# Keys and values ahead of the queries, swaps between query units, angle reduction on GpSimd

## The chip, the cores and the metric

The kernel runs on one core of a Trainium2 chip. The metric is the device time of one execution in microseconds (us); several executions are timed and the median is given. The core has TensorE (PE in the rows; matmuls and, as PEld, weight loads), VectorE (DVE), ScalarE (ACT), GpSimd (POOL), SyncE (SP, whose queue here only issues transfers), and 16 DMA engines between HBM and the on-chip SBUF. TensorE writes to PSUM; no instruction of GpSimd in this kernel has an operand there.

## The reference, cut to what matters

Two transformer blocks on 256 tokens of width 1024, all in float32. The first block is a latent attention plus gated convolution, then a mixture of 32 experts; the second is a recurrent layer, a stick-breaking attention, an MLP and a gate. Only the attention of the first block is touched:

```python
z = hp @ w_in
c_q, c_kv, k_pe, gate_b, gate_c, x_in = jnp.split(z, SPLITS, axis=-1)
q = (rms_norm(c_q, q_norm) @ w_uq).reshape(bsz, plen, N_HEADS, QK_NOPE + QK_ROPE)   # 8 heads, 64 + 32
q_rope = apply_rope(q[..., QK_NOPE:], cos[:, :, None, :], sin[:, :, None, :])
kv = (rms_norm(c_kv, kv_norm) @ w_ukv).reshape(bsz, plen, N_HEADS, QK_NOPE + V_DIM) # 64 + 64
k_nope, v = kv[..., :QK_NOPE], kv[..., QK_NOPE:]
k_rope = apply_rope(k_pe, cos, sin)
attn = causal_block_attention(q_nope, q_rope, k_nope, k_rope, v)
```

cos and sin are those of position times frequency, for 16 frequencies and 272 positions (16 meta tokens and 256 tokens).

## The kernel before, in words

Every engine runs its own program in order; semaphores order the engines against each other. There is no planner: the order of work on each engine is written out by hand.

Weights come as slabs of up to 1 MB into a ring of 12 SBUF slots, in the order of the list SLABS1 (SP's queue, L443 to L462). A slab is cut into units. For each unit ScalarE copies the weights rounded to fp32r into WH (`high1`, L613), VectorE writes the remainder into WL (`low1`, L1061), and TensorE multiplies high by high, high by low and low by high (`triple`, L1741 to L1743). There are four unit buffers, so `high1` of a unit waits until TensorE has used the unit four before it. The result of a unit lies in a PSUM bank, `bank1`, and ScalarE takes it out (`take1`, L626). A column unit holds 128x1024 weights and takes 24 matmuls; a query unit holds one head, 128x192, and takes 6.

The first 8 units are columns of w_in: 0 and 1 are c_q, 2 is c_kv, 3 is k_pe, 4 to 7 are gate_c. Before, units 8 to 15 are the eight query heads and unit 16 is w_ukv. After them the units WOVEN (17) and up, the rest of w_in, are woven into the attention loop.

The order around the change, before:

- TensorE: units 0 to 7 (L1803), among them the matmul of the rope angles into PSUM bank 6 (L1807) and the swap of k_pe (L1818). Then the eight query units (L1822), `swap_queries(0)` (L1838: a matmul with a signed permutation of the rope halves for two heads, L1835), the key matmuls of heads 0 to 3, swaps 1 to 3, the keys of heads 4 to 7, three value tiles (L1860 to L1862), and the attention loop (L1905 to L1921).
- ScalarE: the takes of units 4 to 7, the sine table load and `rope_table(0)` (L695) inside them, then eight times `high1` and take of a query head with `rope_table(1)` in front of the third take, then eight copies of keys (L721), three of values (L725), then the exponentials.
- VectorE: `low1` of the units; `reduce_angle(0)` (L1151 to L1159: eight small instructions on 32x272, each waiting for the one before it) between `low1(5)` and `low1(6)`; the two norms; `low1` up to 10; `reduce_angle(1)`; `low1` of 11 to 16; the rope of the keys into all eight heads (L1186 to L1189); then `rope_queries(j)` (L1202 to L1204), one for each pair of heads, with `low1(WOVEN)` to `low1(WOVEN+2)` and the first steps of the softmax (L1248 to L1256) between them.
- GpSimd: constants and small transfers in its first 14 us, then nothing until the attention is done (L560).

Of the kernel before, what the change touches and what calls it, by code (L numbers as in the profile page):

```python
# [11 lines left out]
ALU = mybir.AluOpType  # L12
# [41 lines left out]
SLABS1 = [("cq", 2), ("kv", 2), ("gc0", 2), ("gc1", 2), ("uq", 8), ("ukv", 1),  # L54
# [12 lines left out]
def bank1(u_no):  # L67

    return u_no % 4 if u_no < WOVEN else 2 + u_no % 2
# [51 lines left out]
def build(nc, A, out):  # L121

    ctx = ExitStack()
    with ctx:
# [7 lines left out]
        def const(name):  # L132
# [4 lines left out]
            vector=("router_low", "kpe_sines", "mix_root", "ffn_in_root", "logits_by_feature", "group_centred", "chosen_ready", "pair_diff",  # L137
                    "overflow_known", "lambda_abs", "ple_root"),
            scalar=("router_high", "mix_std", "group_exp", "pair_exp", "lambda_exp"),
# [100 lines left out]
        ang_k = ar(5520, T)  # L240

# [266 lines left out]
        def _(pool):  # L508
# [35 lines left out]
            g.memset(rank_or[:], -1.0).then_inc(ev("pool_const"), 1)  # L544
            pool.dma_start(gain_pc[:], A["pre_ffn_norm"][0].rearrange("(p c) -> p c", c=DC))\
# [6 lines left out]
            for name, n in VEC2:  # L552
                v = A[name] if name == "norm_final_g_2" else A[name][0]
                if len(v.shape) == 2:
                    v = v.rearrange("k n -> (k n)")
                pool.dma_start(vrow2[row:row + n, :], v.rearrange("(c p) -> c p", p=P)).then_inc(ev("vec2_loaded"), 16)
                row += n

# [42 lines left out]
        def _(act):  # L601
# [59 lines left out]
            for t in range(TT):  # L661
# [4 lines left out]
                if t == 0:  # L666
                    act.wait_ge(ev("meta_square"), 1)
                    s.activation(xs(1, 2)[0:META, :], xs(0, 2)[0:META, :], ACT.Sqrt, scale=1.0 / D, bias=EPS)\
                        .then_inc(ev("meta_std"), 1)
# [9 lines left out]
            for k, dst in enumerate((cq[:, 0, :], cq[:, 1, :], ckv, kpe)):  # L679
# [8 lines left out]
                if k == 2:  # L688
                    root_of_mean("cq", S)
# [8 lines left out]
            for k in range(4):  # L698
# [5 lines left out]
                if k == 1:  # L704
                    rope_table(0)
# [3 lines left out]

            u0 = FIRST1["uq"]  # L710
            for k in range(HEADS):
                high1(u0 + 3 + k)
                if k == 2:
                    rope_table(1)
                take1(u0 + k, qcat[0:QD, k, :], rows=QD, n=S, scale=SCALE1)

            for h in range(HEADS):
                act.wait_ge(ev("nope_keys"), h + 1)
                if h == 0:
                    act.wait_ge(ev("rope_table"), 2)  # L720
# [5 lines left out]
            high1(WOVEN + 2)  # L726
# [318 lines left out]
        def _(dve):  # L1045
# [56 lines left out]
            def scaled(srcs, gains, n):  # L1102
# [11 lines left out]
                                   ALU.add, xs(0, 2)[0:META, :]).then_inc(ev("meta_square"), 1)  # L1114
            dve.wait_ge(ev("pos_loaded"), 16)
            v.tensor_scalar(pos_row[0:1, META:T], pos_int[0:1, :], float(META), None, ALU.add)\
                .then_inc(ev("pos_ready"), 1)
# [3 lines left out]
            dve.wait_ge(ev("meta_std"), 1)  # L1121
# [15 lines left out]
            two_pi = 2 * math.pi  # L1137
            p1 = 6.28125
            p2 = float(np.float32(np.round((two_pi - p1) * 2 ** 20) / 2 ** 20))
            p3 = two_pi - p1 - p2  # L1140
            magic = 1.5 * 2 ** 23
            lim = 3.1415925
            rows = slice(NOPE, QD)
            angp = ps[rows, 6, 0:T]
            kr_a = rope_a[rows, 0:T]

            def reduce_angle(k):
                dst = (ang_k, ang)[k]
                turn = 0.25 * k
                tmp = rstd[rows, 0:T]  # L1150
                chain(v.tensor_scalar(tmp, angp, 1 / two_pi, turn, ALU.mult, ALU.add))  # L1151
                chain(v.tensor_scalar(tmp, tmp, magic, None, ALU.add))
                chain(v.tensor_scalar(tmp, tmp, -magic, None, ALU.add))
                chain(v.scalar_tensor_tensor(out=dst[rows, :], in0=tmp, scalar=-p1, in1=angp, op0=ALU.mult, op1=ALU.add))
                for part in (p2, p3):
                    chain(v.scalar_tensor_tensor(out=dst[rows, :], in0=tmp, scalar=-part, in1=dst[rows, :],
                                                 op0=ALU.mult, op1=ALU.add))
                chain(v.tensor_scalar(dst[rows, :], dst[rows, :], turn * two_pi, lim, ALU.add, ALU.min))
# [1240 lines left out]
```

## Time and profile before

| | us |
|---|---|
| median of 3 runs | 942.52 |
| lowest and highest of them | 936.86, 943.32 |
| the profiled execution | 943.4 |
| its span, first to last instruction | 941.6 |
| mean granted TensorE clock, as a share of 2.4 GHz | 0.937 |
| TensorE busy | 811.3 |
| VectorE busy | 506.0 |
| ScalarE busy | 380.0 |
| GpSimd busy | 44.4 |

All stretches below are in us from the start of the span. TensorE's busy time is modelled from pipelined matmuls, so an engine shown as busy is not at its peak; idle time is what can be read with confidence.

### The profile page before, as it was taken

What the parts mean: (1) busy time and instruction counts of PE and PEld (TensorE: products, weight loads), DVE (VectorE), ACT (ScalarE), POOL (GpSimd) and SP (SyncE); (2) the same over time, 40 slices, a digit from 0 to 9 for tenths busy, and PEclk for the clock granted to TensorE, in tenths of its full rate; (3) what the DMA queues carried; (4) which work ended last, traced back from release to release, by engine and by line L of the source; (5) the groups of instructions that cost most, each with busy time, mean ns of one, the idle gap of its engine ahead of it and who ended that gap; (6) DMA issues with size and microseconds to landing.
All of it is one profiled execution on the core that took longest, in us unless ns stands there. A gap on an engine that the chain in (4) does not pass through costs nothing.

```text
span 941.6 us, 13290 instructions
## 1 busy us (share of the span) xinstructions
PE 811.3 (86%) x5425; PEld 644.0 (68%) x5425; DVE 506.0 (54%) x826; ACT 380.0 (40%) x629; POOL 44.4 (5%) x108
## 2 busy tenths in 40 slices
PE   6989997896686776659999997799999999999975
PEld 5967786763343332329989875487787999999854
DVE  5786547411110030055936988945677666666655
ACT  5563647210100100046456655535445544444444
POOL 5000020010101101000000000000000000000000
PEclk9998998998987889779999997989999999999988
DMA  9941181399999999995417452055554566665001
GB/s 285 374 153 45 46 334 46 139 409 422 422 422 420 420 422 421 410 333 170 149 64 302 160 202 89 1 201 179 179 179 134 185 193 196 189 191 200 11 0 45
DMA packets 75950, 205.81 MB, mean 219 GB/s; under 512 B 5720, under 2 KB 48896, under 8 KB 63600
## 3 DMA queue, kind: packets, MB, share of 16 engines
q1 hardware_dynamic: 67406, 150.44, 44.7%
q0 software_dynamic: 8480, 54.49, 14.3%
q8 instruction: 45, 0.74, 0.3%
q14 instruction: 17, 0.14, 0.0%
q10 hardware_dynamic: 2, 0.00, 0.0%
HBM read 203.87 MB, written 1.05 MB: 218 GB/s over the span
## 4 chain that ended last, share of the span: by engine, by line
PE 62%; DMA 16%; DVE 14%; ACT 4%; issue 2%; SPq 0%; POOL 0%; ACTq 0%; DVEq 0%
DMA big<-in_w_up 16%; PE ps L1938 8%; PE ps L1939 8%; PE ps L1940 8%; PE ps L1741 8%; PE ps L1743 7%; PE ps L1742 7%; PE ps L2052 4%; DVE WL L1069 2%; PE ps L2031 1%; DVE XT L1558 1%; DVE WL L1061 1%; DVE big L1600 1%; ACT WH L622 1%; PE ps L2066 1%
## 5 line engine op out<-in xcount | busy, mean ns | idle before, releaser
L1069 DVE TENSOR_TENSOR WL<-big,WH 128x1024 fp32r<-128x1024 f32 x154 | 186.8, 1224 | 111.8 <-ACT WH L622 110.2
L622 ACT ACTIVATE WH<-big 128x1024 fp32r<-128x1024 f32 x154 | 160.7, 1054 | 89.0 <-PE ps L1940 88.5
L1741 PE MATMUL ps<-XH,WH 128*128 128x256 f32 (+1 forms) x640 | 187.5, 293 | 1.0 <-DVE WL L1061 0.7
L1743 PE MATMUL ps<-XH,WL 128*128 128x256 f32 (+1 forms) x640 | 183.1, 286 | 0.0
L1742 PE MATMUL ps<-XL,WH 128*128 128x256 f32 (+1 forms) x640 | 183.1, 286 | 0.0
L1741 PEld LDWEIGHTS ps<-XH,WH 128*128 128x128 f32 x640 | 123.7, 193 | 6.6 <-issue 4.5
L2052 PE MATMUL ps<-big 128*32 128x256 f32 x1024 | 77.8, 470 | 55.1 <-DMA big<-in_w_gate 33.3
L1742 PEld LDWEIGHTS ps<-XL,WH 128*128 128x128 f32 x640 | 123.8, 194 | 0.8
L1743 PEld LDWEIGHTS ps<-XH,WL 128*128 128x128 f32 x640 | 123.6, 193 | 0.0
L2052 PEld LDWEIGHTS ps<-big 128*32 128x32 f32 x1024 | 42.8, 135 | 92.0 <-issue 81.9
L1938 PE MATMUL ps<-WH,XH 128*128 128x512 f32 x240 | 96.6, 402 | 5.6 <-DVE WL L1069 2.1
L1940 PE MATMUL ps<-WL,XH 128*128 128x512 f32 x240 | 94.9, 396 | 0.0
L1939 PE MATMUL ps<-WH,XL 128*128 128x512 f32 x240 | 94.9, 396 | 0.0
L1449 DVE TENSOR_TENSOR big<-big,ps 128x256 f32<-128x256 f32 x8 | 3.4, 421 | 132.3 <-ACT big L851 132.3
L1938 PE MATMUL ps<-WH,HH 128*128 128x512 f32 x152 | 60.0, 395 | 1.7 <-DVE HL L1697 1.7
L1939 PE MATMUL ps<-WH,HL 128*128 128x512 f32 x152 | 59.4, 391 | 0.0
L1940 PE MATMUL ps<-WL,HH 128*128 128x512 f32 x152 | 59.3, 390 | 0.0
L1938 PEld LDWEIGHTS ps<-WH,XH 128*128 128x128 f32 x240 | 46.0, 192 | 17.6 <-issue 2.6
L1061 DVE TENSOR_TENSOR WL<-big,WH 128x1024 fp32r<-128x1024 f32 (+1 forms) x39 | 40.3, 1045 | 25.9 <-ACT WH L613 25.8
L1940 PEld LDWEIGHTS ps<-WL,XH 128*128 128x128 f32 x240 | 45.9, 191 | 9.9
L1939 PEld LDWEIGHTS ps<-WH,XL 128*128 128x128 f32 x240 | 46.0, 192 | 9.2
L1011 ACT ACTIVATE HH<-big 128x256 fp32r<-128x256 f32 x32 | 13.4, 417 | 76.2 <-DVE big L1694 76.2
(399 smaller groups left out, 1091.7 us busy)
## 6 DMA issues: line engine op xcount, KB each, us to landing
big<-in_w_in SPq DMA_DIRECT2D x35, 1024.0 KB, 9.2
big<-in_w_gate SPq DMA_DIRECT2D x16, 1024.0 KB, 17.1
big<-in_w_up SPq DMA_DIRECT2D x16, 1024.0 KB, 18.2
big<-in_w_gate POOLq DMA_DIRECT2D x16, 1024.0 KB, 19.4
big<-in_w_up POOLq DMA_DIRECT2D x16, 1024.0 KB, 20.1
big<-in_w_down SPq DMA_DIRECT2D x16, 1024.0 KB, 18.6
big<-in_w_down POOLq DMA_DIRECT2D x16, 1024.0 KB, 21.2
big<-in_w_mlp_up SPq DMA_DIRECT2D x16, 1024.0 KB, 5.5
```

The source lines that it names most:

```text
L622: s.activation(dst, src, ACT.Copy).then_inc(ev("unit_high"), 1)
L1011: s.activation(HH[:, f % 2, :], zx[:, f % 2, :], ACT.Copy).then_inc(ev("relu_high"), 1)
L1061: v.tensor_tensor(dst, src, h.bitcast(F32), ALU.subtract).then_inc(ev("unit_split"), 1)
L1069: v.tensor_tensor(dst, src, h.bitcast(F32), ALU.subtract).then_inc(ev("unit_split"), 1)
L1558: chain(v.reciprocal(xt, xt))
L1741: mm(o, h, rh, start=first, stop=False, skip_group_check=skip)
L1742: mm(o, h, rl, start=False, stop=False, skip_group_check=skip)
L1743: return mm(o, l, rh, start=False, stop=last, skip_group_check=skip)
L1938: mm(o, h, WH[:, b, w], start=first, stop=False, skip_group_check=skip)
L1939: mm(o, l, WH[:, b, w], start=False, stop=False, skip_group_check=skip)
L1940: return mm(o, h, WL[:, b, w], start=False, stop=last, skip_group_check=skip)
L2052: last = mm(ps[j * CAP:(j + 1) * CAP, 1, up * FF:(up + 1) * FF], x(c)[:, j * CAP:(j + 1) * CAP], slot(first_slot + j)[:, c * FF:(c + 1) * FF],
```

## The change

The slab w_ukv moves ahead of w_uq: it is now unit 8 and the query heads are units 9 to 16. `bank1` follows.

- TensorE: after unit 7 the keys of all eight heads and the three value tiles. Head h < 4 waits for the take of unit 4 + h. Then the eight query units; swaps 0, 1 and 2 follow query units 3, 5 and 7; swap 3 follows the first four chunks of the woven unit.
- ScalarE: one new copy of the angles from PSUM bank 6 to SBUF (32x272) ahead of the first square root of a norm. Both rope tables, with the sine table load, now follow the take of unit 7. Then one `high1`, the eight key copies, the three value copies, then eight times `high1` and take of a query head (the last three of the `high1` are those of WOVEN to WOVEN+2).
- VectorE: both `reduce_angle` are gone. The rope of the keys stands ahead of `low1` of query units 2 to 7 and follows `low1` of unit 10.
- GpSimd: both `reduce_angle`, in the stretch where it had nothing to do. Each of VectorE's three fused steps (scalar_tensor_tensor) is written as a tensor_scalar and a tensor_tensor: 11 instructions for each of the two, 8 tensor_scalar and 3 tensor_tensor, each waiting for the one before it.
- Several semaphores are merged into the marks of their engines; the waits stay.

```diff
-SLABS1 = [("cq", 2), ("kv", 2), ("gc0", 2), ("gc1", 2), ("uq", 8), ("ukv", 1),
+SLABS1 = [("cq", 2), ("kv", 2), ("gc0", 2), ("gc1", 2), ("ukv", 1), ("uq", 8),
...
-    return u_no % 4 if u_no < WOVEN else 2 + u_no % 2
+    return u_no % 4 if u_no < FIRST1["ukv"] else (u_no + 2) % 4 if u_no < WOVEN else 2 + u_no % 2
...
+            def reduce_angle(k):
+                dst, tmp = (ang_k, ang)[k][rows, :], ang_turns[rows, :]
+                turn = 0.25 * k
+                chain(g.tensor_scalar(tmp, ang_whole[rows, :], 1 / two_pi, turn, ALU.mult, ALU.add))
+                chain(g.tensor_scalar(tmp, tmp, magic, None, ALU.add))
+                chain(g.tensor_scalar(tmp, tmp, -magic, None, ALU.add))
+                chain(g.tensor_scalar(ang_part[rows, :], tmp, -p1, None, ALU.mult))
+                chain(g.tensor_tensor(dst, ang_part[rows, :], ang_whole[rows, :], ALU.add))
+                for part in (p2, p3):
+                    chain(g.tensor_scalar(ang_part[rows, :], tmp, -part, None, ALU.mult))
+                    chain(g.tensor_tensor(dst, ang_part[rows, :], dst, ALU.add))
+                chain(g.tensor_scalar(dst, dst, turn * two_pi, lim, ALU.add, ALU.min))
+                g.tensor_scalar(dst, dst, -lim, None, ALU.max).then_inc(ev("angle_reduced"), 1)
...
+            pool.wait_ge(*mark("angles_kept"))
+            reduce_angle(0)
+            reduce_angle(1)
...
                 take1(k, dst)
                 if k == 2:
+                    act.wait_ge(*mark("angles"))
+                    s.activation(ang_whole[NOPE:QD, :], ps[NOPE:QD, 6, 0:T], ACT.Copy).then_inc(ev("scalar_mark"), 1)
                     root_of_mean("cq", S)
...
-                if k == 1:
-                    rope_table(0)
...
+            rope_table(0)
+            rope_table(1)
             u0 = FIRST1["uq"]
-            for k in range(HEADS):
-                high1(u0 + 3 + k)
-                if k == 2:
-                    rope_table(1)
-                take1(u0 + k, qcat[0:QD, k, :], rows=QD, n=S, scale=SCALE1)
-
+            high1(u0 + 2)
             for h in range(HEADS):
                 act.wait_ge(ev("nope_keys"), h + 1)
...
-            high1(WOVEN + 2)
+            for k in range(HEADS):
+                high1(u0 + 3 + k)
+                take1(u0 + k, qcat[0:QD, k, :], rows=QD, n=S, scale=SCALE1)
...
-            for k in range(1, 6):
+            for k in range(1, 7):
                 low1(k)
-            dve.wait_ge(*mark("angles"))
-            reduce_angle(0)
-            low1(6)
...
-            reduce_angle(1)
-            u0 = FIRST1["uq"]
-            for k in range(6):
-                low1(u0 + 3 + k)
...
+            for k in range(2, HEADS):
+                low1(u0 + k)
...
+            for k in range(HEADS):
+                pe.wait_ge(ev("unit_split"), u0 + k + 1)
+                if 1 <= k < 4:
+                    pe.wait_ge(ev("values_ready"), k)
+                elif k >= 4:
+                    pe.wait_ge(*taken1(u0 + k - 4))
+                columns((u0 + k) % NB, bank1(u0 + k), HH, HL, S, chunks=2, step=QD).then_inc(ev("unit_used"), 1)
+                if k in (3, 5, 7):
+                    swap_queries((k - 3) // 2)
...
+            pe.wait_ge(*taken1(u0 + 7))
             scores(0)
             woven_unit(WOVEN, 0, 4)
+            swap_queries(3)
             scores(1)
```

## Rows read from the trace of the kernel before

**Rows 1.** The page: span, and the chain that ended last by engine.

```profile
span 941.6 us, 13290 instructions
...
PE 62%; DMA 16%; DVE 14%; ACT 4%; issue 2%; SPq 0%; POOL 0%; ACTq 0%; DVEq 0%
```

**Rows 2.** Windows: stretch, length, busy us by engine, granted clock, DMA share, GB/s.

```profile
75.00:80.00 5.00, 5.00 (x23) 3.78 (x21) 3.28 (x7) 1.51 (x5) 0.00 (x0) 0.56 0.14 57
80.00:85.00 5.00, 5.00 (x30) 4.06 (x29) 1.30 (x8) 1.85 (x9) 0.00 (x0) 0.76 0.00 0
```

**Rows 3.** Timeline, TensorE: start, us, instruction, count, [idle before, releaser].

```profile
46.16 0.39 PE L1741 MATMUL ps<-HH,WH 128*128 128x256 f32 x1 [1.46 <-DVE WL L1061]
...
49.86 1.02 PE L1835 MATMUL ps<-big,swap 96*96 96x512 f32 x2
52.08 0.36 PE L1741 MATMUL ps<-sel,WH 128*128 128x272 f32 x1 [1.20 <-ACT big L626]
...
59.86 0.41 PE L1876 MATMUL ps<-big 96*128 96x144 f32 x2
...
65.11 0.40 PE L1741 MATMUL ps<-XH,WH 128*128 128x272 f32 x1 [0.70 <-DVE WL L1061]
...
69.35 0.44 PE L1888 MATMUL ps<-ident,big 128*128 128x128 f32 x2 [2.00 <-DVE big L1256]
...
74.31 0.33 PE L1888 MATMUL ps<-ident,big 128*128 128x128 f32 x1 [1.75 <-DVE big L1256]
```

**Rows 4.** Timeline, VectorE, from the second angle reduction to the first softmax step.

```profile
42.56 0.44 DVE L1151 TENSOR_SCALAR rstd<-ps 32x272 f32<-32x272 f32 x1
...
45.42 0.29 DVE L1159 TENSOR_SCALAR big<-big 32x272 f32<-32x272 f32 x1
...
51.35 2.42 DVE L1189 TENSOR_TENSOR big<-big 32x2176 f32<-32x2176 f32 x1
53.80 0.69 DVE L1202 TENSOR_TENSOR big<-ps,sin_t 32x512 f32<-32x512 f32 x1
...
60.30 0.32 DVE L1248 CUSTOM_DVE_ANT_0 ps<-ps,masks 128x144 f32<-128x144 f32 x1 [0.97 <-PE ps L1876]
```

**Rows 5.** Timeline, ScalarE: root, table load, sine, take of unit 7, copies.

```profile
26.46 0.39 ACT L640 ACTIVATE std<-ps 128x256 f32<-128x256 f32 x1 [0.18 <-PE ps L1781]
...
38.50 1.28 ACT L695 ACT_TABLE_LOAD   x1
39.79 0.43 ACT L695 ACTIVATE sin_t<-big 32x272 f32<-32x272 f32 x1
...
42.60 0.40 ACT L626 ACTIVATE big<-ps 128x272 f32<-128x272 f32 x1 [1.12 <-PE ps L1743]
42.90 0.35 ACT L613 ACTIVATE WH<-big 128x192 fp32r<-128x192 f32 x1
...
52.73 1.52 ACT L721 ACTIVATE big<-ps 64x272 f32<-64x272 f32 x4 [0.79 <-PE ps L1743]
...
58.66 2.00 ACT L725 ACTIVATE hT<-ps 128x512 f32<-128x512 f32 x3 [0.30 <-PE ps L1862]
```

**Rows 6.** Timeline, GpSimd: a memset, two affine selects.

```profile
1.27 0.33 POOL L513 MEMSET masks<- 128x272 f32 x1
...
1.53 0.20 POOL L514 MEMSET big<- 1x128 f32 x1
...
1.97 0.29 POOL L516 TENSOR_SCALAR_AFFINE_SELECT ident<-ident 128x128 f32<-128x128 f32 x1 [0.24 <-POOL big L514]
...
121.25 1.02 POOL L566 TENSOR_SCALAR_AFFINE_SELECT masks<-masks 128x128 f32<-128x128 f32 x1
```

**Rows 7.** Groups of instructions, VectorE, 26.5 to 42.5: busy us, mean ns.

```profile
L1061 DVE TENSOR_TENSOR WL<-big,WH 128x1024 fp32r<-128x1024 f32 x2 | 2.5, 1225 | 0.6 <-ACT WH L613 0.5
...
L1104 DVE SCALAR_TENSOR_TENSOR XT<-big,vec,rstd 128x256 f32<-128x256 f32 x2 | 0.9, 480 | 0.0
...
L1084 DVE TENSOR_TENSOR HL<-XT,HH 128x256 fp32r<-128x256 f32 x2 | 0.8, 425 | 0.1
```

More of the change, by code:

```diff
@@ L544, in _, with chain @@
             g.memset(rank_or[:], -1.0).then_inc(ev("pool_const"), 1)
+            rows = slice(NOPE, QD)
+            angle_steps = [0]
+            def chain(ins):
+                angle_steps[0] += 1
+                ins.then_inc(ev("angle_step"), 1)
+                pool.wait_ge(ev("angle_step"), angle_steps[0])
+            two_pi = 2 * math.pi
+            p1 = 6.28125
+            p2 = float(np.float32(np.round((two_pi - p1) * 2 ** 20) / 2 ** 20))
+            p3 = two_pi - p1 - p2
+            magic = 1.5 * 2 ** 23
+            lim = 3.1415925
+            def reduce_angle(k):
[11 more added lines that the diff above has]
+                g.tensor_scalar(dst, dst, -lim, None, ALU.max).then_inc(ev("angle_reduced"), 1)
             pool.dma_start(gain_pc[:], A["pre_ffn_norm"][0].rearrange("(p c) -> p c", c=DC))\
@@ L1136, in _ @@
                     .then_inc(ev("x_low"), 1)
[L1137 to L1142, printed above, removed]
             rows = slice(NOPE, QD)
-            angp = ps[rows, 6, 0:T]
             kr_a = rope_a[rows, 0:T]
[L1147 to L1158, printed above, removed]
-                v.tensor_scalar(dst[rows, :], dst[rows, :], -lim, None, ALU.max).then_inc(ev("angle_reduced"), 1)
-            for k in range(1, 6):
+            for k in range(1, 7):
                 low1(k)
-            dve.wait_ge(*mark("angles"))
-            reduce_angle(0)
-            low1(6)
             root("cq", S)
@@ L1171, in _ @@
             split("ckv", scaled([ckv], [g1("kv_norm")], T), [KL[:, 0:T]], T, [KH[:, 0:T]])
-            for k in range(8, 11):
+            u0 = FIRST1["uq"]
+            for k in range(8, u0 + 2):
                 low1(k)
@@ L1818, in _ @@
                     mm(ps[0:QD, 5, 0:T], swap[:], kpe[0:QD, :], start=True, stop=True).then_inc(ev("tensor_mark"), 1)
[L1820 to L1840 removed]
+            u0, uk = FIRST1["uq"], FIRST1["ukv"]
             pe.wait_ge(ev("unit_split"), uk + 1)
@@ L1848, in _ @@
                     pe.wait_ge(ev("nope_keys_taken"), h - 3)
+                else:
+                    pe.wait_ge(*taken1(uk - 4 + h))
                 w = slice(h * NOPE, h * NOPE + P)
@@ L1864, in _, with swap_queries @@
             pe.wait_ge(ev("nope_keys_taken"), HEADS)
+            def swap_queries(j):
+                pe.wait_ge(*taken1(u0 + 2 * j + 1))
+                if j == 0:
+                    pe.wait_ge(ev("vecs_ready"), 2)
+                if j == 1:
+                    pe.wait_ge(*mark("kpe_sines"))
+                if j == 2:
+                    pe.wait_ge(*mark("angles_kept"))
+                if j == 3:
+                    pe.wait_ge(ev("std_ready"), 2)
+                mm(ps[0:QD, 4 + j, :], swap[:], qcat[0:QD, 2 * j:2 * j + 2, :].rearrange("p h t -> p (h t)"),
+                   start=True, stop=True).then_inc(ev("q_swapped"), 1)
+            pe.wait_ge(ev("split_low"), SP_AT["cq"] + 2)
+            for k in range(HEADS):
[7 more added lines that the diff above has]
+                    swap_queries((k - 3) // 2)
             def scores(n):
@@ L1871, in scores @@
                 if n < 2:
[L1872 removed]
+                    pe.wait_ge(*mark("rope_keys"))
                     pe.wait_ge(ev("q_roped"), n + 1)
```

48 lines of the change are left out of this document (12 added, 36 removed).

## The prediction

> **What bounds the kernel now.** I read the chain that ended last first: TensorE holds 62% of it, VectorE 14%, ScalarE 4%, and GpSimd nothing [rows 1]. The change lies between the end of column unit 7 (about 42.4 us) and the start of the attention loop (about 60 us). All that comes after hangs on the attention through TensorE, so a microsecond won or lost at the loop's start should reach the end whole, unless the stages behind it are limited by something that doesn't move.
>
> I then read TensorE's timeline for its idle time, which alone can be won. It is 1.46 us before the fourth query unit, waiting for a VectorE remainder; 1.20 us before the keys, waiting for ScalarE's take of the last query head; then 0.70, 2.00 and 1.75 us at the start of the loop, all waiting for VectorE [rows 3]. Together that is 7.1 us. The first wait is the change's target: the second angle reduction sits on VectorE from 42.56 to 45.71 [rows 4], with the remainder of a query unit queued behind it.
>
> The decisive view is VectorE's. From 53.80 it works on the rope of the queries without a pause, stops 0.97 us for the first scores at 60.30 [rows 4], and works on until 69 us (rope of pairs 2 and 3, two remainders, softmax steps). The idle 0.70, 2.00 and 1.75 us of TensorE lie in and behind that. So the loop's start is a VectorE chain, and what the change is worth is read from when its two ends come: the first rope of queries (53.80) and the first softmax step (60.30).
>
> **The change, part by part.**
>
> *The fold leaves VectorE.* Eight instructions, 3.15 us, twice. The first lies under TensorE's column units, which ran without a gap, so it is worth nothing while units 6 and 7 have their weights in time. The second frees VectorE at 41.5, but its next item, the rope of the keys, now waits for ScalarE's tables. It is worth nothing by itself either.
>
> *ScalarE's new chain.* ScalarE waited for TensorE and took unit 7 at 42.60, its next instruction began at 42.90 [rows 5]. That stays. Before, the table load of 1.28 us lay at 38.50 under units 6 and 7; now it stands behind the take, on the path. From 42.90: load 1.28, two tables at 0.43 with some 0.03 between them, so 45.10; one small high1, 0.3 (45.4); eight key copies at 1.52/4 = 0.38 (48.45) [rows 5]. TensorE makes keys 0 to 3 at 42.5 to 44.0, idles until the first copy at about 45.8 (1.8 us, new), and stays one copy ahead from then on. The three values take TensorE about 0.7 each, three times, from 47.4 to 49.5: before, the first value copy began at 58.66 [rows 5] and the scores, queued behind two more values, at 59.86 [rows 3]. ScalarE's three value copies, 2.00/3 = 0.67 each, end at about 50.4.
>
> *The queries.* A query unit costs TensorE (49.86 - 46.16)/5 = 0.74 [rows 3]. Units 0 to 2 follow the values from 49.5; unit 3 waits for the third value copy (50.4) and for its own weights, rounded only after that copy (0.3, and 0.35 on VectorE: 51.1), then for unit 2, and ends at 52.3. Swap 0, two passes, took 1.02 alone [rows 3]: 53.3. VectorE has ended the rope of the keys (2.42, from about 45.9) at 48.3 and the last query remainder at about 53.4, since ScalarE comes to that unit's high1 only after take 3 at 52.7. So the first rope of queries starts at about 53.5 against 53.80: no gain, as ScalarE's queue is now the limit.
>
> *The first softmax step.* VectorE goes on: rope of pair 0 (2.1), remainder of WOVEN (its high1 ends about 55.3 on ScalarE, in time), rope of pair 1 (2.1): free at about 59.05. TensorE: query units 4 to 7 and swaps 1 and 2 end at about 57.9; ScalarE's takes and three large high1 of 1.05 end with the last take at 58.3; scores 0 at 58.4. VectorE no longer waits: the first softmax step starts at 59.05 against 60.30, **1.25 us earlier**. Behind it both queues hold the same work in the same order, so the 0.70, 2.00 and 1.75 us stay and only move. Swap 3, 1.0 us, now lies in the loop's first unit, where TensorE idles more than that.
>
> *ScalarE's copy of the angles* (0.3) comes at 26.5, in front of the root at 26.46 [rows 5]. VectorE gets unit 6 and the root in about the old time, as its own 3.15 us ahead of them are gone. Cost: nothing. Without that cover it is 0.3 us of a chain that has 3 us of slack to the queries.
>
> *Transfers.* The 0.5 MB slab of w_ukv is asked for in front of w_uq, some 25 us before its use. The last slab of the ring goes out about 8 us earlier, the first expert slab about 3 us later; both are used after 140 us. Nothing.
>
> *GpSimd.* The trace has none of these instructions on GpSimd, so I bound them. Below: a write of 272 columns takes 0.26 (from 1.27 to the next start at 1.53), and a wait between two dependent instructions 0.24 [rows 6]: 22 x 0.50 = 11 us. Above: an affine select of 128 columns took 1.02 [rows 6]; for 272 that is 2.17, with the wait 2.4, times 22 = 53 us. I take the value nearest to the memset, the plain stream: one pass for each operand read or written. A tensor_scalar is 2 x 0.26 + 0.24 = 0.76, a tensor_tensor 3 x 0.26 + 0.24 = 1.02: 16 x 0.76 + 6 x 1.02 = 18.3 us. Started at 26.8, done at 45.1. The second table wants it at 44.65: **0.4 us late**. Who stands behind this wait matters: all of ScalarE's chain above, thus keys, values, queries, one for one.
>
> Sum: -1.25 + 0.4 = about -0.9 us. Against the profiled execution's 943.4 this gives 942.5; against the median of 942.52, which lies 0.9 below it, 941.6.
>
> The Trainium skill, GPSIMD Engine Reference, section 3.1, gives about 2.6 cycles an element for a two-input add on GpSimd, and puts its clock at 1.2 GHz; by that page's figures an estimate of the tensor_tensor stream is 0.59 us against my 0.78, and the fold would be done by some 1 us sooner. No row here shows it.
>
> **The rivals.**
>
> *A. GpSimd and VectorE exclude each other.* In GpSimd's stretch VectorE runs remainders and norm steps with two SBUF inputs: three large remainders (one more than before, as w_ukv is a large unit) at 1.225, and 0.9 and 0.8 for the norm's pairs: 5.4 us [rows 7]. If GpSimd stands still in each, it ends at 50.5, 5.8 us after ScalarE wants it. Then the time is -1.25 + 5.8 = 4.6 us up: 947.1. It decides from the point where GpSimd ends later than 45.9, that is 0.87 us an instruction; this is the rival on the other side. For it: those instructions fill much of the stretch. Against it: they can also overlap only in part, and VectorE may be the one that waits, with slack. The Trainium skill, SBUF — State Buffer, section "Who interferes with whom", says just this: a VectorE instruction with two SBUF inputs and a GpSimd one that reads SBUF shut each other out for a whole instruction. No row of before has the two side by side.
>
> *B. GpSimd is far slower*, towards 2.4 us an instruction: done at 80, ScalarE's chain 35 us late, 976. It is the affine select's price. A simple multiply has no comparison by position, and the select at 1.97 shows 0.29 [rows 6], so this is unlikely. At 1.3 us an instruction it is 10 us late and just over 1% slower.
>
> *C. The clock.* Behind the idle 2.00 and 1.75 us TensorE's granted clock falls to half (1.2 GHz): 0.56 of full over 75 to 80 and 0.76 over 80 to 85, with TensorE busy throughout [rows 2]. That makes (0.44 + 0.24) x 5 = 3.4 us of lost clock. The same gaps come 0.9 us earlier, so I expect it again. If it stays away: 941.6 - 3.4 = 938.2. If another comes, as much up.
>
> *D. The gain is lost* by a limit that doesn't move, for instance a transfer: 942.5.
>
> **How the numbers follow.** Forecast (about 1 us down) 0.45; A 0.23; B, all of it, 0.10; C in either sense 0.12; D 0.10. Predicted is the likeliest, 941.6. About 1%, 9.4 us, is what a measurement of this kernel can tell from no change. Faster by more needs all the idle time at the loop and the clock at once: 0.03. Slower by more needs B from 1.3 us an instruction: 0.10. The rest, 0.87, is the same. The range takes in C and the spread of the runs of before downwards (they reach 936.9), and A with some more upwards, and leaves out most of B: 935 to 950.
>
> **What would show it.** VectorE has no L1151 to L1159 any more; GpSimd has 22 instructions from about 26.8. If they end by 45 and the cosine table starts at 44.7, the GpSimd step is right; ScalarE idle ahead of that table shows A or B, with its size. The table load at 42.9 and a gap of 1.8 us on TensorE before key 4 show the new chain. The first rope of queries at 53.5 and the first softmax step at 59.05, no longer waiting for scores, show the sum. Low clock at another place or none shows C. I would be wrong if ScalarE's chain is shorter than its parts, or the idle time inside the loop goes too.

## The result

The changed kernel takes 947.9 us (median of 8 runs, 946.38 to 951.3) against 941.55 us for the kernel before (8 runs): a ratio of 1.0072, with a 95% interval of 1.0056 to 1.0089. It is 6.35 us slower by the medians. The forecast was 0.9 us faster; the time lies inside the stated range. That it comes near rival A's 947.1 is luck, as the account of the prediction below shows.

The page of the changed kernel, its span and its busiest engines (busy us, share of the span, instructions), and the chain that ended last:

```profile
span 945.2 us, 13296 instructions
PE 812.8 (86%) x5425; PEld 645.4 (68%) x5425; DVE 501.3 (53%) x810; ACT 380.2 (40%) x630; POOL 65.6 (7%) x130
...
PE 60%; DMA 17%; DVE 13%; ACT 4%; POOL 3%; issue 2%; SPq 0%; DVEq 0%; ACTq 0%; POOLq 0%
```

GpSimd, which held nothing of the chain before [rows 1], now holds 3% of it. That is about 28 us (0.03 x 945) with a rounded share; the two reductions take 23.2 of them. The waits of the changed kernel between 42 and 75 us, longest first (who waited for whom: total us, times, longest), say who stood behind it:

```profile
DVE big L1192 <- ACT cos_t L733: 8.9, 1, 8.9
PEld ps L1749 <- ACT big L752: 7.4, 1, 7.4
PE ps L1749 <- ACT big L752: 7.1, 1, 7.1
ACT cos_t L733 <- POOL big L574: 5.3, 1, 5.3
```

Read from below: ScalarE's cosine table waited 5.3 us for GpSimd's last instruction; TensorE waited 7.1 us for the key copy that is queued behind that table (some 1.7 us of this wait also stands in e3_early_copy, where GpSimd is in time); VectorE waited 8.9 us for the table itself. ScalarE's timeline of the changed kernel shows the place (as in [rows 5]):

```profile
43.28 0.40 ACT L662 ACTIVATE big<-ps 128x272 f32<-128x272 f32 x1 [2.04 <-PE ps L1751]
43.70 1.28 ACT L733 ACT_TABLE_LOAD   x1
44.99 0.42 ACT L733 ACTIVATE sin_t<-big 32x272 f32<-32x272 f32 x1
50.74 0.43 ACT L733 ACTIVATE cos_t<-big 32x272 f32<-32x272 f32 x1 [5.33 <-POOL big L574]
51.19 0.36 ACT L649 ACTIVATE WH<-big 128x192 fp32r<-128x192 f32 x1
```

The take, the table load and the sine table follow each other just as predicted. The whole execution runs 0.7 us later than the one of before by then, so the take of unit 7 starts at 43.28 instead of 42.60. To be free of that offset, I measure a stretch from here on: **from the start of ScalarE's take of unit 7 to the start of VectorE's first softmax step**. Before it was 60.30 - 42.60 = 17.70 us [rows 4, 5]. The prediction made it 59.05 - 42.60 = 16.45, plus 0.4 for GpSimd. In the changed kernel the step starts at 67.30, on VectorE's timeline, and the stretch is 24.02 us, 6.3 more than before:

```profile
51.27 0.44 DVE L1192 TENSOR_TENSOR big<-ps,sin_t 32x272 f32<-32x272 f32 x1 [8.90 <-ACT cos_t L733]
...
61.73 0.69 DVE L1210 TENSOR_TENSOR big<-ps,sin_t 32x512 f32<-32x512 f32 x1
...
67.30 0.32 DVE L1256 CUSTOM_DVE_ANT_0 ps<-ps,masks 128x144 f32<-128x144 f32 x1
```

That is as much as the loss of 6.35 in the medians, but the agreement is in part chance. In the two profiled executions the last softmax step of the attention comes 70.9 us after the take of unit 7 instead of 66.7 (109.25 - 42.60 before, 114.21 - 43.28 changed), 4.3 more, and the spans differ by 3.6 (945.2 and 941.6). What lies behind the stretch thus moves the end by some us of its own.

GpSimd's timeline of the changed kernel, the second reduction from its second instruction on; VectorE ran its last instruction at 41.93 to 42.37 and then nothing until 51.27, so the rows from 43.20 on are GpSimd alone:

```profile
27.55 0.41 POOL L565 TENSOR_SCALAR big<-big 32x272 f32<-32x272 f32 x1 [13.53 <-ACT big L726]
...
29.05 1.67 POOL L567 TENSOR_SCALAR big<-big 32x272 f32<-32x272 f32 x1
...
40.10 1.74 POOL L566 TENSOR_SCALAR big<-big 32x272 f32<-32x272 f32 x1
41.92 1.20 POOL L567 TENSOR_SCALAR big<-big 32x272 f32<-32x272 f32 x1
43.20 0.89 POOL L568 TENSOR_SCALAR big<-big 32x272 f32<-32x272 f32 x1
44.17 0.76 POOL L569 TENSOR_TENSOR big<-big 32x272 f32<-32x272 f32 x1
...
48.62 1.12 POOL L573 TENSOR_SCALAR big<-big 32x272 f32<-32x272 f32 x1
49.82 0.89 POOL L574 TENSOR_SCALAR big<-big 32x272 f32<-32x272 f32 x1
```

The 22 instructions run from 27.55 to 50.71: 23.2 us instead of the 18.3 of the prediction. The table wanted the angles at 45.41, when the sine table was done.

### The profile page after: what moved, and what is told of

The parts are those of the page before. It is cut to its first block, busy times and chain, and to the rows that moved or that the text cites. A ratio compares the mean times of both kernels' runs of the same rounds, so it can differ in the third digit from the quotient of the medians.

```text
span 945.2 us, 13296 instructions
## 1 busy us (share of the span) xinstructions
PE 812.8 (86%) x5425; PEld 645.4 (68%) x5425; DVE 501.3 (53%) x810; ACT 380.2 (40%) x630; POOL 65.6 (7%) x130
## 3 DMA queue, kind: packets, MB, share of 16 engines
HBM read 203.87 MB, written 1.05 MB: 217 GB/s over the span
## 4 chain that ended last, share of the span: by engine, by line
PE 60%; DMA 17%; DVE 13%; ACT 4%; POOL 3%; issue 2%; SPq 0%; DVEq 0%; ACTq 0%; POOLq 0%
DMA big<-in_w_gate 15%; PE ps L1949 8%; PE ps L1950 8%; PE ps L1951 8%; PE ps L1749 8%; PE ps L1751 7%; PE ps L1750 7%; PE ps L2063 4%; DMA big<-in_w_in 3%; DVE WL L1102 2%; DVE big L1608 1%; PE ps L2042 1%; DVE XT L1566 1%; ACT WH L658 1%; DVE WL L1094 1%
## 5 line engine op out<-in xcount | busy, mean ns | idle before, releaser
L2063 PE MATMUL ps<-big 128*32 128x256 f32 x1024 | 79.8, 480 | 53.3 <-DMA big<-in_w_gate 34.8
```

Source lines behind the costliest of these rows:

```text
L2063: last = mm(ps[j * CAP:(j + 1) * CAP, 1, up * FF:(up + 1) * FF], x(c)[:, j * CAP:(j + 1) * CAP], slot(first_slot + j)[:, c * FF:(c + 1) * FF],
```

## The experiments

Each was timed in the same session as the kernel before; "before" is that session's median, and ratios have their 95% interval. The ratio is not the quotient of the two medians and can differ from it by up to 0.0012. Every diff is against the changed kernel, other than that of e5_old_order_late_copy. The stretch is the one defined above, from the profiled execution.

| | time, us | before | ratio | stretch, us |
|---|---|---|---|---|
| before | | | | 17.70 |
| changed | 947.9 | 941.55 | 1.0072 (1.0056 to 1.0089) | 24.02 |
| e1_vector_fold | 940.32 | 941.68 | 0.9979 (0.9963 to 0.9994) | 16.74 |
| e2_short_fold | 939.94 | 941.68 | 0.9989 (0.9974 to 1.0003) | 16.54 |
| e3_early_copy | 941.13 | 941.68 | 0.9993 (0.9977 to 1.0009) | 16.55 |
| e4_early_copy_and_table | 941.43 | 941.68 | 0.9997 (0.9978 to 1.0016) | 16.46 |
| e5_old_order_late_copy | 944.76 | 942.68 | 1.0019 (1.0000 to 1.0038) | 22.02 |
| e6_old_order_early_copy | 941.29 | 942.68 | 0.9995 (0.9978 to 1.0012) | 16.11 |
| e7_pair_form | 942.39 | 942.68 | 0.9997 (0.9978 to 1.0016) | 16.82 |
| e8_all_early | 940.82 | 942.68 | 0.9974 (0.9954 to 0.9995) | 14.59 |
| e9_idle_work | 947.69 | 940.63 | 1.0063 (1.0043 to 1.0083) | 18.31 |
| e10_busy_wait | 946.32 | 940.63 | 1.0057 (1.0035 to 1.0078) | 22.03 |
| e11_changed_again | 947.37 | 940.63 | 1.0062 (1.0041 to 1.0084) | 23.41 |

### e1_vector_fold: the order without GpSimd

```diff
             pool.wait_ge(*const("rank_or"))
-            pool.wait_ge(*mark("angles_kept"))
-            reduce_angle(0)
-            reduce_angle(1)
...
-            for k in range(1, 7):
+            for k in range(1, 6):
                 low1(k)
+            dve.wait_ge(*mark("angles"))
+            reduce_angle(0)
+            low1(6)
...
                 .then_inc(ev("vector_mark"), 1)
+            reduce_angle(1)
```

> The changed order of all queues is kept, but the two angle reductions are VectorE's again, at their old places (ahead of the remainder of unit 6, and behind the router's remainder), and ScalarE's copy of the angles is gone. Theory W (the loss is ScalarE's 5.3 us wait for GpSimd's last instruction, and the half clock of TensorE that follows it): the cosine table starts at about 45.6 instead of 50.7, the first softmax step at about 59.5, and the time is 940.5, 1 below before and 7.4 below the changed kernel. Rival O (the new order itself costs, as the queries come last and the table load is on the path): the time stays above 944.

Measured: 940.32 us, ratio 0.9979, 1.4 us under before; the cosine table started at 44.23, on time, and the stretch was 16.74 us. With the reductions back on VectorE all of the loss is gone, and the new order is slightly better than the old one. Rival O (the new order itself costs) falls. Its stretch is 0.2 us longer than that of the next two, since VectorE's second reduction ends last in front of the cosine table.

### e2_short_fold: the order when the angles are never late

```diff
-                chain(g.tensor_scalar(tmp, tmp, magic, None, ALU.add))
-                chain(g.tensor_scalar(tmp, tmp, -magic, None, ALU.add))
-                chain(g.tensor_scalar(ang_part[rows, :], tmp, -p1, None, ALU.mult))
-                chain(g.tensor_tensor(dst, ang_part[rows, :], ang_whole[rows, :], ALU.add))
-                for part in (p2, p3):
-                    chain(g.tensor_scalar(ang_part[rows, :], tmp, -part, None, ALU.mult))
-                    chain(g.tensor_tensor(dst, ang_part[rows, :], dst, ALU.add))
+                chain(g.tensor_tensor(dst, tmp, ang_whole[rows, :], ALU.mult))
```

> The changed kernel with only 4 instead of 11 instructions in each of GpSimd's two reductions; the range reduction of the angles is left out by that, all else is the same work. Theory W: GpSimd is done at about 35, no wait for it is left, cosine table at about 45.3, first softmax step at about 59.3, time 940.3. Rival O: above 944. It also shows what the order is worth when the angles are never late.

Measured: 939.94 us, ratio 0.9989, and a stretch of 16.54 us, against 16.45 in the prediction's sum without GpSimd's delay. So the chain worked out for ScalarE, TensorE and VectorE was right to 0.1 us as a whole; a part of it was off by more (the eight key copies took 2.63 us instead of 3.04). On the time, the 1.7 us between the medians are not resolved, as the interval of the ratio reaches 1.0003.

### e3_early_copy: the same reduction, begun 7 us earlier

```diff
                 high1(k + 3)
+                if k == 1:
+                    act.wait_ge(*mark("angles"))
+                    s.activation(ang_whole[NOPE:QD, :], ps[NOPE:QD, 6, 0:T], ACT.Copy).then_inc(ev("scalar_mark"), 1)
                 if k < 3:
...
                 if k == 2:
-                    act.wait_ge(*mark("angles"))
-                    s.activation(ang_whole[NOPE:QD, :], ps[NOPE:QD, 6, 0:T], ACT.Copy).then_inc(ev("scalar_mark"), 1)
                     root_of_mean("cq", S)
```

> The changed kernel with ScalarE's copy of the angles moved from behind the take of unit 2 to the front of the square of unit 1, where ScalarE is idle for 2.2 us; GpSimd starts its 22 instructions about 7 us earlier. Theory W: it starts at about 20.5 and ends at about 44, just in time for the cosine table at 45.3: time 940.5. Rival X (GpSimd and VectorE exclude each other so much that more of VectorE's remainders in the stretch eat the lead): it ends at 47 or later, time 943 or more, and units 2 to 7 may leave TensorE idle.

Measured: 941.13 us, ratio 0.9993. GpSimd's first and last instruction, and ScalarE's cosine table:

```profile
20.16 1.10 POOL L565 TENSOR_SCALAR big<-big 32x272 f32<-32x272 f32 x1 [6.11 <-ACT big L719]
...
42.93 0.89 POOL L574 TENSOR_SCALAR big<-big 32x272 f32<-32x272 f32 x1
```

```profile
43.86 0.41 ACT L734 ACTIVATE cos_t<-big 32x272 f32<-32x272 f32 x1
```

GpSimd ran from 20.16 to 43.82, 23.7 us, and was 0.04 us ahead of the cosine table at 43.86. The stretch is 16.55 us, that of e2_short_fold. So one moved copy of 0.39 us takes back the loss of the changed kernel with all 22 instructions still on GpSimd. GpSimd did need 0.5 us more here than in the changed kernel, with more of VectorE's work beside it, but rival X's 47 us did not come. The end time is within its interval of before; the 1.15 us that the stretch is shorter can't be told from it.

### e4_early_copy_and_table: the table load off the path

The edit of e3_early_copy, and:

```diff
+                if k == 1:
+                    rope_table(0)
                 if k == 2:
                     act.wait_ge(ev("router_loaded"), 64)
...
-            rope_table(0)
             rope_table(1)
```

> As e3_early_copy, and the sine table with its table load of 1.28 us back to its old place behind the take of unit 5, off the path. Theory W with ScalarE's chain as the limit behind the take of unit 7: that chain is 1.7 us shorter if the cosine angles are there by 43.6; GpSimd ends at about 44, so 1.3 us of it are seen: time 939.2, about 1.3 below e3_early_copy. If VectorE or TensorE limits the stretch, it is no faster than e3_early_copy.

Measured: 941.43 us, ratio 0.9997, stretch 16.46 us. I had expected 1.3 us less than e3_early_copy and got 0.1 on the stretch and nothing on the time. ScalarE's timeline shows where the freed time went:

```profile
38.79 1.28 ACT L734 ACT_TABLE_LOAD   x1
40.09 0.43 ACT L734 ACTIVATE sin_t<-big 32x272 f32<-32x272 f32 x1
...
42.47 0.40 ACT L662 ACTIVATE big<-ps 128x272 f32<-128x272 f32 x1 [0.70 <-PE ps L1753]
44.41 0.42 ACT L734 ACTIVATE cos_t<-big 32x272 f32<-32x272 f32 x1 [1.54 <-POOL big L574]
```

The load and the sine table left the path, and a wait of 1.54 us for GpSimd took their place, which ended at 44.38. GpSimd began at 20.82 and needed 23.6 us. The expectation was off at both ends: counted from the take of unit 7, GpSimd was done 0.5 us later than it had reckoned (1.9 us behind the take instead of 1.4), and the cosine table of e3_early_copy had already been 0.7 us earlier (2.0 behind it instead of 2.7).

### e5_old_order_late_copy and e6_old_order_early_copy: GpSimd without the new order

Both have the queues of before, except that the reductions are GpSimd's; they differ only in the place of ScalarE's copy. This diff is against the kernel before.

```diff
+            pool.wait_ge(*mark("angles_kept"))
+            reduce_angle(0)
+            reduce_angle(1)
...
-            for k in range(1, 6):
-                low1(k)
-            dve.wait_ge(*mark("angles"))
-            reduce_angle(0)
-            low1(6)
+            for k in range(1, 7):
+                low1(k)
...
-            reduce_angle(1)
             u0 = FIRST1["uq"]
```

> One part alone: the order of before on every engine, but both angle reductions on GpSimd, fed by ScalarE's copy behind the take of unit 2, as in the changed kernel. Theory W: GpSimd ends at about 50; ScalarE wants the cosine table at 43.9 in front of the take of the third query head, so it waits some 6 us there, and the queries behind it: time about 945 to 947. Rival: only the new order of keys and queries makes the wait expensive, then the time is that of before, 941.7.

> As e5_old_order_late_copy, with ScalarE's copy in front of the square of unit 1. GpSimd ends at about 44, just when the cosine table is wanted. VectorE is free of its 3.15 us at 42.6, the fourth query unit no longer waits 1.46 us: first softmax step about 1.2 us earlier than before, time 940.4. If the time VectorE gives up is worth nothing on the path, it is 941.7.

Measured: 944.76 us with the late copy, ratio 1.0019 (1.0000 to 1.0038), and 941.29 with the early one, 0.9995. The late copy's cosine table waited 4.33 us for GpSimd, TensorE idled 3.81 us in front of a query unit behind it, and the stretch is 22.02 us, 4.3 longer than before. So GpSimd alone, without the new order, is enough for most of the loss in the stretch. At the end of the program I had expected 3 to 5 us and saw 2.1, just at the edge of what the interval tells from nothing. In the profiled executions 2.9 of the 4.3 us are left at the last softmax step of the attention (111.98 - 42.48 against 109.25 - 42.60); why the rest is gone is not shown, and the clock behind the stretch (below) differs from run to run. With the early copy the stretch is 16.11, 1.6 shorter than before: in the old order, too, VectorE's freed 3.15 us are worth something, in the stretch even more than the new order (1.0 in e1_vector_fold). On the time the interval, 0.9978 to 1.0012, can't tell it from nothing.

### e7_pair_form: what sets GpSimd's price

The rows of the changed kernel had a surprise: of the tensor_scalar the one with multiply and add (L565) took 0.41 us, those with one operation 0.89, more than a tensor_tensor with its two inputs (0.76).

```diff
-                chain(g.tensor_scalar(tmp, tmp, magic, None, ALU.add))
-                chain(g.tensor_scalar(tmp, tmp, -magic, None, ALU.add))
-                chain(g.tensor_scalar(ang_part[rows, :], tmp, -p1, None, ALU.mult))
+                chain(g.tensor_scalar(tmp, tmp, 1.0, magic, ALU.mult, ALU.add))
+                chain(g.tensor_scalar(tmp, tmp, 1.0, -magic, ALU.mult, ALU.add))
+                chain(g.tensor_scalar(ang_part[rows, :], tmp, -p1, 0.0, ALU.mult, ALU.add))
...
-                    chain(g.tensor_scalar(ang_part[rows, :], tmp, -part, None, ALU.mult))
+                    chain(g.tensor_scalar(ang_part[rows, :], tmp, -part, 0.0, ALU.mult, ALU.add))
```

> The changed kernel with the same 22 instructions on GpSimd, but the 12 tensor_scalar that have one operation and no second are written with two (times 1 or times the constant, then plus the magic number or plus 0). In the trace of the changed kernel the one tensor_scalar with multiply and add took 0.41 us, those with one operation 0.88 to 0.92 where VectorE was idle. If the form sets the price, each of the 12 falls to about 0.5 with its wait, GpSimd needs about 18 us instead of 23.2 and ends at about 46, the wait of 5.3 us on ScalarE is nearly gone, time 940.8. If the price is the columns or the hand-over between dependent instructions, nothing changes: 947.9.

(Ten instructions are changed by this, five in each reduction; the expectation says twelve.) Measured: 942.39 us, ratio 0.9997: the loss is gone, though not the 940.8 that were expected. GpSimd's timeline of e7_pair_form, start and end:

```profile
26.40 0.41 POOL L565 TENSOR_SCALAR big<-big 32x272 f32<-32x272 f32 x1 [12.35 <-ACT big L726]
26.89 0.41 POOL L566 TENSOR_SCALAR big<-big 32x272 f32<-32x272 f32 x1
27.39 0.41 POOL L567 TENSOR_SCALAR big<-big 32x272 f32<-32x272 f32 x1
...
42.19 1.22 POOL L573 TENSOR_SCALAR big<-big 32x272 f32<-32x272 f32 x1
43.48 0.89 POOL L574 TENSOR_SCALAR big<-big 32x272 f32<-32x272 f32 x1
```

The same columns, the same waits, the same place: 0.41 instead of 0.92 and more, 18.0 us in all instead of 23.2. It ends at 44.37 and the cosine table starts at 44.40, still some 0.2 us late (2.28 us behind the take of unit 7 instead of 2.04). What made the single operations dear is the form of the instruction, neither the columns nor the hand-over, which is the 0.08 to 0.09 between rows.

### e8_all_early: a version faster than both

e3_early_copy with the two-operation form and both tables behind the take of unit 5.

```diff
+                if k == 1:
+                    rope_table(0)
+                    rope_table(1)
...
-            rope_table(0)
-            rope_table(1)
```

> The changed order with the early copy, the two-operation form on GpSimd, and both tables behind the take of unit 5, all off the path. If GpSimd ends before 39, ScalarE's chain behind the take of unit 7 is shorter by 1.28 + 2 x 0.45 = 2.2 us than in e3_early_copy, and the first softmax step comes that much earlier: time 938.5 to 939. If something else (TensorE's values, VectorE) limits the stretch, it is 940 to 941.

Measured: 940.82 us against 942.68, ratio 0.9974 (0.9954 to 0.9995): 1.9 us by the medians, 2.5 by the ratio, where 2.7 to 3.2 was expected. The two-operation form ended GpSimd's work at 39.53; ScalarE's rows have both tables ahead of unit 7's take at 41.86 and the first key copy right behind it:

```profile
37.77 1.28 ACT L734 ACT_TABLE_LOAD   x1
39.07 0.43 ACT L734 ACTIVATE sin_t<-big 32x272 f32<-32x272 f32 x1
39.57 0.43 ACT L734 ACTIVATE cos_t<-big 32x272 f32<-32x272 f32 x1
...
42.51 2.77 ACT L754 ACTIVATE big<-ps 64x272 f32<-64x272 f32 x8
```

The stretch is 14.59 us, 3.1 shorter than before, and TensorE no longer idles in front of the fifth key head.

### e9_idle_work: do GpSimd and VectorE share something?

The edit of e3_early_copy, and:

```diff
             reduce_angle(0)
             reduce_angle(1)
+            spare = hT[:].rearrange("p c t -> p (c t)")[rows, 1536:2080].rearrange("p (b t) -> p b t", b=2)
+            chain(g.memset(spare[:, 0, :], 1.0))
+            chain(g.memset(spare[:, 1, :], 1.0))
+            pool.wait_ge(*mark("rope_keys"))
+            for _ in range(24):
+                chain(g.tensor_scalar(spare[:, 0, :], spare[:, 0, :], 1.0, None, ALU.mult))
+                chain(g.tensor_tensor(spare[:, 1, :], spare[:, 0, :], spare[:, 1, :], ALU.mult))
```

> e3_early_copy with 48 more instructions on GpSimd (24 tensor_scalar and 24 tensor_tensor on 32x272, in the spare end of the tile that holds the values, results unused), begun when the keys have their rope, so that they run against VectorE's busiest stretch, some 54 to 97. Theory X (GpSimd and VectorE instructions with two SBUF inputs shut each other out): VectorE's rope steps with two SBUF inputs, 0.68 us before, grow by some tenths, those that read PSUM stay at 0.69, GpSimd's get up to 1 us longer in places; VectorE is the path there, so the first softmax steps come 1 to 3 us later and the time is 942 to 944. If they run side by side at full speed, the time is that of e3_early_copy, 941, and no duration moves.

Measured: 947.69 us, ratio 1.0063, where 942 to 944 was expected; nobody waits for the added instructions. The groups of VectorE instructions between 52 and 100 us (count, then busy us and mean ns), first of e3_early_copy:

```profile
L1211 DVE TENSOR_TENSOR big<-ps,sin_t 32x512 f32<-32x512 f32 x4 | 2.8, 688 | 0.1
L1212 DVE TENSOR_TENSOR big<-big,cos_t 32x512 f32<-32x512 f32 x4 | 2.7, 683 | 0.1
L1213 DVE TENSOR_TENSOR big<-big 32x512 f32<-32x512 f32 x4 | 2.7, 682 | 0.1
```

and the same three of e9_idle_work:

```profile
L1221 DVE TENSOR_TENSOR big<-big 32x512 f32<-32x512 f32 x4 | 4.7, 1162 | 0.1
...
L1220 DVE TENSOR_TENSOR big<-big,cos_t 32x512 f32<-32x512 f32 x4 | 3.7, 914 | 0.1
L1219 DVE TENSOR_TENSOR big<-ps,sin_t 32x512 f32<-32x512 f32 x4 | 2.8, 689 | 0.1
```

The step that reads one operand from PSUM didn't move (688 and 689 ns). The two with both operands in SBUF grew from 683 to 914 and from 682 to 1162. VectorE's tensor_scalar, with its one tensor in SBUF, grew too, from 362 to 496 ns in the softmax on 272 columns. GpSimd's own rows show the other side: its tensor_scalar is 0.88 where it runs free and 1.21 or 1.74 in places. So the two engines do hold each other up, and in these rows only where VectorE reads nothing from PSUM.

How far they do so can be read where two begin together. GpSimd's rows of e9_idle_work, then VectorE's:

```profile
54.91 0.88 POOL L600 TENSOR_SCALAR hT<-hT 32x272 f32<-32x272 f32 x1
55.87 0.76 POOL L601 TENSOR_TENSOR hT<-hT 32x272 f32<-32x272 f32 x1
```

```profile
54.94 0.92 DVE L1220 TENSOR_TENSOR big<-big,cos_t 32x512 f32<-32x512 f32 x1
55.89 1.29 DVE L1221 TENSOR_TENSOR big<-big 32x512 f32<-32x512 f32 x1
```

Beside the tensor_scalar VectorE lost 0.24 us (0.92 - 0.68) of the 0.88, beside the tensor_tensor 0.61 (1.29 - 0.68) of the 0.76. So the one that comes second does not wait for the whole of the first. The stretch grew by 1.8 us over e3_early_copy, within the expectation. Against their own before the two kernels stand at +7.1 and -0.5 us by the medians, so most of the 7.6 between them came behind the first softmax step, where the added work still ran until 99 us; the expectation had not counted it. From the first to the last softmax step of the attention it is 52.5 us (61.54 to 114.03) against 48.9 (58.37 to 107.24), 3.6 more. TensorE's clock was 0.83, 0.84 and 0.65 over 60 to 70, 70 to 80 and 80 to 90, against 1.00, 0.69 and 0.97, which is 3.4 us of lost clock more. How much of the 3.6 is this clock and how much the longer VectorE instructions is not shown, and the last 2.2 of the 7.6 are not placed.

### e10_busy_wait and e11_changed_again: is the half clock part of the loss?

```diff
+                if h == 4:
+                    pe.wait_ge(ev("std_ready"), 2)
+                    for _ in range(48):
+                        mm(ps[:, 7, 0:T], WH[:, b, 0:P], KH[:, 0:T], start=True, stop=True)
                 if h >= 4:
                     pe.wait_ge(ev("nope_keys_taken"), h - 3)
```

> The changed kernel with 48 matmuls of 272 columns, results unused, in front of the keys of head 4, where TensorE sat idle for 7.1 us. They fill about 6 us of the wait and add none to it. Theory T (the wait costs 5.3 us, and some 2 us more because TensorE's clock is at half behind it, so that keys 4 to 7 and the first values run at 0.68 us instead of 0.38 a head): the clock stays full there, and the time is about 2 us below the changed kernel, 946. If the half clock costs nothing on the path, the time stays at that of the changed kernel.

> The changed kernel once more, unedited, beside the other two on the same chip, as their yardstick: 947.5, some 6 us above before; GpSimd's 22 instructions take 23 us again, ScalarE waits 5.3 us.

In the changed kernel the matmuls behind the 7.13 us of idle time run slower. Its timeline on TensorE:

```profile
51.89 0.59 PE L1749 MATMUL ps<-sel,WH 128*128 128x272 f32 x1 [7.13 <-ACT big L752]
52.28 0.43 PE L1750 MATMUL ps<-sel,WH 128*128 128x272 f32 x1
52.51 0.43 PE L1751 MATMUL ps<-sel,WL 128*128 128x272 f32 x1
```

They start 0.23 apart instead of 0.13, and a key head takes 0.68 us instead of 0.38. The windows from 50 to 60 us (busy us by engine, then the granted clock, the DMA share and GB/s) of the changed kernel, 0.68, and of e10_busy_wait, 1.00:

```profile
50.00:60.00 10.00, 8.11 (x41) 7.53 (x42) 4.37 (x7) 6.71 (x19) 0.71 (x1) 0.68 0.41 150
```

```profile
50.00:60.00 10.00, 9.22 (x60) 8.11 (x61) 6.72 (x11) 8.31 (x24) 0.00 (x0) 1.00 0.47 160
```

In e10_busy_wait the key heads start 0.38 apart again, and ScalarE still waits for GpSimd:

```profile
49.64 0.42 ACT L733 ACTIVATE cos_t<-big 32x272 f32<-32x272 f32 x1 [5.37 <-POOL big L574]
```

Its stretch is 22.03 us: 1.4 shorter than that of e11_changed_again in the same session (23.41, with a clock of 0.82 over 50 to 60) and 2.0 shorter than in the first profile (24.02, with 0.68). Against e2_short_fold, the same order without the wait, e10_busy_wait is 22.03 - 16.54 = 5.5 us longer, which is the wait. The changed kernel is 24.02 - 16.54 = 7.5 us longer in the first profile and 23.41 - 16.54 = 6.9 in the second: the wait of 5.3, and 1.4 to 2.0 of half clock. On the time, e10_busy_wait gives 946.32 against 947.37, 1.05 us less, with intervals of the ratios that overlap (1.0035 to 1.0078 and 1.0041 to 1.0084). The half clock is shown in the stretch; its share of the end time isn't resolved.

## Why the prediction was wrong

**The step that failed is one term of the sum**, GpSimd's 18.3 us, which measured 23.2: the cosine table came 5.3 us late instead of 0.4, and the sign turned with it. Who waits for it was stated rightly, and that the forecast turns from the point where GpSimd ends later than 45.9. That the delay passes one for one held only with TensorE's clock kept full (5.4 us of wait, 5.5 in the stretch of e10_busy_wait); in the changed kernel a half clock that the sum had not counted came on top.

- *The order of the queues: right.* The first softmax step 1.25 us earlier if the angles are in time: 16.45 us predicted, 16.54 measured in e2_short_fold. That the gain is to be read from VectorE's chain, and not from the 1.46 and 1.20 us that TensorE idles, was right too: in that kernel VectorE works from the first rope of queries at 53.88 to the softmax step at 59.44 without a pause.
- *GpSimd's price: mis-sized.* I built it from a memset: one pass of 0.26 us for each operand, 0.76 for a tensor_scalar and 1.02 for a tensor_tensor. Measured alone, with the hand-over (start to start), it is 0.97 for one with a single operation, 0.50 for multiply and add, 1.20 for add and minimum, 0.85 for a tensor_tensor. One reduction is 0.50 + 5 x 0.97 + 3 x 0.85 + 1.20 + 0.97 = 10.1 us, two 20.1: 1.8 us over the prediction. The guess had even the order wrong: the two-input instruction is the cheaper one. An instruction that no row shows needs a bound at which the forecast holds; here the forecast hung on 0.87 us an instruction, beside an estimate of 0.83, and that margin should have moved the chances.
- *Exclusion: put in a rival, and real, but not whole.* The other 23.2 - 20.1 = 3.1 us are GpSimd held up by VectorE: single rows of 1.67, 1.75, 1.74 and 1.20 instead of 0.89, each of which runs beside a VectorE instruction with two SBUF inputs. I allowed 5.4 us for rival A. The three large remainders cost GpSimd 0.8 to 0.9 each, less than their 1.23; beside the norm's pairs it lost only some 0.3, and VectorE was the one that waited (1.39 us for two scalings that took 0.88 in the profile of before).
- *Rival A's time came out by luck.* Its 947.1 rests on 5.4 us of exclusion; measured were 3.1 of exclusion, 1.8 of a mis-sized price, and a half clock that it did not have.
- *The rule on exclusion.* The rule of the Trainium skill (SBUF — State Buffer, section "Who interferes with whom") that a VectorE instruction with two SBUF inputs contends with a GpSimd instruction that reads SBUF is borne out by e9_idle_work: 682 to 1162 ns with two SBUF inputs, 688 to 689 with one and PSUM. That they shut each other out for a whole instruction, as the prediction has it, is not what the rows show: 0.24 us lost beside a tensor_scalar of 0.88. The prediction gave rival A 0.23; with a rule that speaks to just this case and no row against it, it should have been in the forecast.
- *The figure of the Trainium skill*, GPSIMD Engine Reference, section 3.1, gives an estimate of 0.59 us for a tensor_tensor's stream; the row has 0.76 with whatever else belongs to the instruction. Both are below the 0.78 of the prediction for the stream, and neither was what decided.
- *The clock: the wrong place.* Rival C looked at the half clock behind the loop's first units. The loss of 1.4 to 2.0 us in the stretch came from a new one, over keys 4 to 7 and the first values, behind the idle 7.1 us. A wait of 5.3 us cost 6.9 to 7.5. The forecast had no such gap, but rival A had one of 5.8 us and put no clock on it. When a delay leaves TensorE idle for that long, the slower matmuls behind it belong into its price.
- *The sum, as it came out:* -1.2 (order) + 5.3 (GpSimd, of which I had 0.4) + 1.4 to 2.0 (clock) = 5.5 to 6.1 us in the stretch. Measured there were 6.3 in the first profile and 5.7 in e11_changed_again (23.41 - 17.70); at the end 6.35.
- *That a microsecond at the loop's start reaches the end whole: open.* The medians lost 6.35 us for 6.3 in the stretch, but in the two profiled executions 4.3 of the 6.3 are left at the last softmax step, and in e5_old_order_late_copy 2.9 of 4.3.
- *Transfers, the first reduction, ScalarE's extra copy at nothing:* right. Units 2 to 7 ran without a gap as before; the take of unit 7 is 0.7 us later than in the profile of before because the whole execution is (the remainder of unit 5 at 24.89 against 24.22).

## What to carry to other kernels

Work moved to an idle engine is free only while that engine delivers before the first wait for it: work out the instruction price at which it turns, and if it lies near the estimate, give the work more lead first. Here one copy of 0.39 us, moved into a gap of ScalarE 7 us earlier, was worth the whole loss. Look for who is queued behind the waiting instruction: a table that only VectorE needed in a hurry stood ahead of ScalarE's key copies, and so stopped three engines.

## What the runs showed of the hardware

- On GpSimd, at 32x272 float32, a tensor_scalar with multiply and add took 0.41 us, one with a single operation 0.88 to 0.89, add and minimum 1.12, a tensor_tensor 0.76. Giving a single operation a neutral second one halved it (e7_pair_form).
- GpSimd and VectorE lengthen each other's instructions when both of VectorE's inputs are in SBUF: 682 to 1162 ns and 683 to 914, and also with a tensor_scalar of VectorE on one tensor in SBUF, 362 to 496; with nothing on one that reads PSUM (688 to 689). The second to begin is not held for the whole of the first: it lost 0.24 us beside a tensor_scalar of 0.88 and 0.61 beside a tensor_tensor of 0.76 (e9_idle_work).
- Behind 7.1 us without a matmul TensorE's granted clock was at half, 1.2 GHz: a key head cost 0.68 us instead of 0.38, in both profiles of the changed kernel. With matmuls in that gap it stayed at 2.4 GHz (e10_busy_wait). In e5_old_order_late_copy it was 0.66 of full over 50 to 60 us, behind 3.81 us of idle time.
- The half clock behind the loop's first units [rows 2] came in nearly every profile: 0.69 to 0.84 of full clock over 70 to 80 us. In the profiled execution of e1_vector_fold alone it was 1.00 from 40 to 90, and that one had the shortest span of all profiled executions, 934.3 us (a time of 936.08), against a median time of 940.32. Single executions of one kernel lie several us apart here (936.08 to 943.21 in e1_vector_fold), more than most of the differences measured above; only the medians of many carry them.
